# A hybrid decoder step on one core: the reload of keys and queries ahead of the last cached key pages, and the recurrence's operands loaded one a step

## The chip, the cores and the metric

The kernel runs on one core of one Trainium2 chip. The metric is the device time of one execution in microseconds. PE is TensorE (matrix multiply), DVE VectorE, ACT ScalarE, POOL GpSimd and SP SyncE; SP and POOL issue nearly all DMA transfers here, each through a queue of its own.

## The reference, cut to what matters

One layer of a decoder for a prompt of 1024 tokens and 8 samples of one token each, model width 1024:

```
x += 0.5 * SwiGLU_1(RMSNorm(x))
P  = RMSNorm(x) @ W_in            # RWKV-7 columns | q, k, v | two branch gates
A  = RWKV7_time_mix(P_rw)         # state recurrence over the tokens
B  = DiffAttn(P_q, P_k, P_v)      # p1 - lambda*p2, rotary, causal
x += (sigmoid(Ga) * (A @ W_pa) + sigmoid(Gb) * (B @ W_pb)) @ W_out
x += 0.5 * SwiGLU_2(RMSNorm(x))

# a sample's attention reads 2048 cached positions through a page table
kp = cache_k[pt].reshape(n_past, 2 * DA_HEADS, DA_QK)
vp = cache_v[pt].reshape(n_past, DA_HEADS, DA_V)
s = einsum("bqhd,bkhd->bhqk", q, k) * DA_QK ** -0.5
```

All is float32. The sample part has 8 samples of 16 pages, each page 128 positions by 512 numbers (256 KB).

## The kernel before, in words

The program is written by hand for each engine; within an engine instructions stand in the order of the code, and engines meet at semaphores. Activations lie transposed, features on the 128 partitions and 1032 tokens (1024 of the prompt, 8 samples) along them.

Three stages matter here. **The unit loop** computes 30 column blocks ("units", `n` = 0 to 29) of `W_in`: 14 for the recurrence, then 16 for the gates. PE fills PSUM for a unit; DVE reads it out (`tmp<-ps,rstd_mix`, L1903) and thereby frees that PSUM half; for a gate unit ACT then applies the sigmoid and POOL stores it (`gate_save`, L915). In the shadow of the same loop DVE works on the samples' attention scores: a group `f` (0 to 31) is four cached key pages. For each group DVE multiplies by the query (`kq_prod<-key_ring`, L1854) and sums (`score_sums<-kq_prod`, L1858), in the function `score_pages`. The key ring holds two groups. SP loads the pages of the groups of unit `n` two passes later (`groups_of(n - 2)`), a group at a time, when the group two before it has been used (`k_used`). `GROUPS_OF` says how many groups each unit has.

During the unit loop POOL also stores what the recurrence will need later (`kk_save`, `b_save`, `kp_save` and others; the last is `kp_save`, L928, of the fourth head pair at `n` = 26). All of these count on `prep_stored`. Their buffers lie where the rotated keys `Kr` and queries `Q` of the prompt must come back, so these two are reloaded (2064 KB each, `k_rot<-k_save` and `q_rot<-q_save`, L704 and L705) only when `prep_stored` is complete.

**Attention** follows: 32 steps, four head pairs for each of 8 query blocks. The first scores on PE (L2646) need `k_back`, `q_back` and both PSUM halves free. DVE first reduces the sample scores over pages (`rstd<-score_sums`, L1935), then takes the maxima of the first step's scores (L1986 to L1989). From step 4 on, PE weights the cached values in between (`weight_values`, L2623), again in groups `f` of four pages in a ring of three, which SP loads (`value_ring` or `tmp<-in_cache_v`, L685).

**The recurrence** follows attention. Its five operands (kk, b, k, r, v; four tiles of 516 KB each, twenty in all) are loaded back by POOL at the opening of attention, and nothing reads them before attention's last steps. `w_trans_lo` counts the steps whose probability transposes PE has done.

Of the kernel before, what the change touches and what calls it, by code (L numbers as in the profile page):

```python
# [30 lines left out]
HP = 4  # L31
# [100 lines left out]


UNITS = ZT + GT
GROUPS_OF = [0 if n == 0 else 2 if n in (15, 20, 26) else 1 for n in range(UNITS)]
HALF_OF = [n for n in range(UNITS) for _ in range(GROUPS_OF[n])]
PREP_AT = [4, 10, 16, 22]

# [90 lines left out]
def build(nc, A):  # L229

    ctx = ExitStack()
    with ctx:
        ev = Events(nc, ctx)
# [18 lines left out]
        def tiles(name, first, n, dt=F32):  # L252

            return at(name, n * NT, arena + first * TILE, dt)[:, :].rearrange("p (k n) -> p k n", n=NT)
# [48 lines left out]
        Q = tiles("q_rot", 0, HP)  # L303
        Kr = tiles("k_rot", 4, HP)
# [31 lines left out]
        Rf, Kf, Vf = tiles("r_mix", 28, HP), tiles("k_new", 12, HP), tiles("v_mix", 36, HP)  # L336
        KKn = tiles("kk", 16, HP)
        Bf = tiles("b_vec", 20, HP)
# [21 lines left out]
        def both_heads(n):  # L360
# [65 lines left out]
        q_save, k_save, r_save, v_save, kk_save, b_save, kp_save, cum_save = [  # L426
            nc.dram_tensor(name + "_save", (HP, P, NT), F32).ap()
            for name in ("q", "k", "r", "v", "kk", "b", "kp", "cum")]
# [41 lines left out]
        def groups_of(n):  # L470

            return [f for f in range(4 * NS) if HALF_OF[f] == n]
# [146 lines left out]
        def _(sp):  # L619
            def load_unit(s, c, src, nk=KT, second=None):  # L620

                sp.wait_ge(*ev.at(f"w_split{s}", c))
                h = HP
                sp.dma_start(stg[s][:, 0:h, :], src[:, 0:h]).then_inc(ev[f"w_loaded{s}"], 16)
                sp.dma_start(stg[s][:, h:nk, :], src[:, h:nk] if second is None else second)\
                    .then_inc(ev[f"w_loaded{s}"], 16)
# [56 lines left out]
            def cache_page(slot, cache, at, done):  # L683
                page = sp.value_load(ptab[0:1, at], min_val=0, max_val=N_PHYS - 1)
                sp.dma_start(slot, cache[ds(page, 1)].rearrange("a t n -> (a t) n")).then_inc(ev[done], 16)  # L685
# [7 lines left out]
            for n in range(UNITS + 2):  # L693
                if n < UNITS:
                    m = Z_ORDER[n] if n < ZT else GT0 + n - ZT
                    load_unit(n % 2, AT_Z + n // 2, wsrc["w_in"][:, :, m * P:(m + 1) * P])
                for f in groups_of(n - 2):
                    if f >= 2:
                        sp.wait_ge(*ev.at(f"k_used{f % 2}", f // 2))
                    for j in range(4):  # L700
                        cache_page(kring[:, f % 2, j, :], ck, slice(4 * f + j, 4 * f + j + 1), f"key_pages{f % 2}")

            sp.wait_ge(*ev.at("prep_stored", 4 * 16 * HP))
            sp.dma_start(Kr, k_save.rearrange("h p n -> p h n")).then_inc(ev["k_back"], 16)  # L704
            sp.dma_start(Q, q_save.rearrange("h p n -> p h n")).then_inc(ev["q_back"], 16)  # L705
            sp.wait_ge(*ev.at("unit_done0", AT_MERGE))
            sp.wait_ge(*ev.at("unit_done1", AT_MERGE))
            for f in range(4 * NS):
# [42 lines left out]
            for t in range(9):  # L751
                sp.wait_ge(*ev.at(f"y_moved{t % 2}", t // 2 + 1))
                dst = A["y_prompt"][0, t * P:(t + 1) * P, :] if t < 8 else A["y_sample"][:, 0, :]
# [6 lines left out]
        def _(pool):  # L760
# [143 lines left out]
            for n in range(UNITS):  # L904
                p, s = n // 2, n % 2
# [36 lines left out]
            pool.wait_ge(*ev.at("z_stored0", 16 * ring_before(ZT)))  # L942
            pool.wait_ge(*ev.at("z_stored1", 16 * ring_before(ZT + 1)))
            pool.wait_ge(*ev.at("z_rows_stored", 32))
            for dst, src, done in ((KKn, kk_save, "kk_back"), (Bf, b_save, "b_back"), (Kf, kp_save, "kp_back"),
                                   (Rf, r_save, "r_back"), (Vf, v_save, "v_back")):
                for h in range(HP):
                    pool.dma_start(dst[:, h, :], src[h]).then_inc(ev[done], 16)

            def now(c):  # L950
# [2097 lines left out]
```

## Time and profile before

| | us |
|---|---|
| median of 3 runs | 2707.53 |
| lowest and highest | 2705.37 and 2708.22 |
| the profiled execution, its time | 2708.39 |
| its span, first to last instruction | 2706.7 |
| PE busy | 2597.7 (96%) |
| DVE busy | 1700.8 (63%) |

The profile page shows PE busy nearly throughout; the stretch with the most room is attention's opening, from about 1276 us of the span. Times in the rows below are microseconds from the span's start.

### The profile page before, as it was taken

The page shows a single profiled execution, that of the slowest core. Times are in us where ns is not written, and L with a number is a line of the kernel's source. Part 1 is how long each engine was busy: PE and PEld are TensorE (multiplying, and loading weights), DVE is VectorE, ACT ScalarE, POOL GpSimd, SP SyncE. Part 2 cuts the span into 40 slices and gives each one's busy share as a digit, 9 for nine tenths or more (in the row PEclk, how much of TensorE's full clock was granted, in tenths as well). Part 3 has the DMA queues.
Part 4 walks back from the last instruction along what each step waited for, and adds up shares of the span by engine and source line. Part 5 has one row for each costly group of instructions (what it writes and reads, how often), then busy time and mean ns, then how long its engine had stood idle before and what let it go on. Part 6 is the DMA issues. An engine that isn't in the chain of part 4 may idle for free.

```text
span 2706.7 us, 55163 instructions
## 1 busy us (share of the span) xinstructions
PE 2597.7 (96%) x22570; PEld 2463.5 (91%) x22570; DVE 1700.8 (63%) x2054; ACT 804.5 (30%) x1321; POOL 593.5 (22%) x534
## 2 busy tenths in 40 slices
PE   7999999999999999998788999979999999999998
PEld 7999999999999999998355899869999999999998
DVE  5877777422484588677766777575487777663223
ACT  6333333111211222332444232221343333331012
POOL 2333332100010232111101655220023333320000
PEclk8999999999999999999799999879999999999999
DMA  5233332751323545667975101043323333236411
GB/s 196 74 116 98 111 106 64 273 181 55 102 94 106 157 142 173 218 203 252 319 212 162 30 26 31 18 147 109 125 75 110 106 98 111 74 107 208 148 48 71
DMA packets 293399, 342.14 MB, mean 126 GB/s; under 512 B 22324, under 2 KB 217744, under 8 KB 293024
## 3 DMA queue, kind: packets, MB, share of 16 engines
q1 hardware_dynamic: 252960, 189.42, 23.6%
q0 software_dynamic: 40000, 149.17, 15.3%
q8 instruction: 177, 2.90, 0.4%
q14 instruction: 70, 0.57, 0.1%
q10 hardware_dynamic: 192, 0.07, 0.0%
HBM read 254.32 MB, written 84.28 MB: 125 GB/s over the span
## 4 chain that ended last, share of the span: by engine, by line
PE 87%; DVE 8%; DMA 1%; ACT 1%; issue 1%; DVEq 0%; SPq 0%; POOL 0%; ACTq 0%
PE ps L2360 43%; PE ps L2488 29%; PE ps L2726 1%; PE ps L2688 1%; PE ps L2646 1%; PE ps L2741 1%; PE ps L2405 1%; PE ps L2746 1%; PE ps L2623 1%; DMA w_stage<-in_ffn_up 1%; PE ps L2580 1%; PE ps L2773 1%; PE ps L2781 1%; ACT w_trans L1422 1%; PE ps L2671 1%
## 5 line engine op out<-in xcount | busy, mean ns | idle before, releaser
L2360 PE MATMUL ps<-h,w_hi 128*128 128x344 f32 x2112 | 506.4, 324 | 0.0
L2360 PEld LDWEIGHTS ps<-h,w_hi 128*128 128x128 f32 x2112 | 362.1, 188 | 17.4 <-issue 16.7
L2360 PE MATMUL ps<-h,w_lo 128*128 128x344 f32 x1056 | 337.2, 319 | 0.0
L1747 DVE SCALAR_TENSOR_TENSOR x_res<-ps,x_res 128x1032 f32<-128x1032 f32 x48 | 59.2, 1233 | 321.0 <-PE ps L2360 321.0
L2488 PE MATMUL ps<-t,w_hi 128*128 128x258 f32 x1408 | 257.4, 284 | 1.0 <-DVE tmp L1689 0.5
L1166 ACT ACTIVATE w_hi<-w_stage 128x512 fp32r<-128x512 f32 x252 | 157.6, 627 | 317.8 <-PE ps L2488 288.5
L2488 PE MATMUL ps<-t_one,w_hi 128*128 128x258 f32 x1280 | 234.4, 285 | 3.1 <-issue 2.5
L2488 PEld LDWEIGHTS ps<-t,w_hi 128*128 128x128 f32 x1408 | 218.2, 190 | 1.5 <-issue 0.7
L1689 DVE TENSOR_TENSOR tmp<-tmp,ps 128x516 f32<-128x516 f32 x210 | 145.4, 692 | 108.4 <-PE ps L2488 95.3
L1658 DVE TENSOR_TENSOR w_lo<-w_stage,w_hi 128x512 fp32r<-128x512 f32 x252 | 192.0, 762 | 22.7 <-ACT w_hi L1166 0.4
L2488 PEld LDWEIGHTS ps<-t_one,w_hi 128*128 128x128 f32 x1280 | 199.2, 191 | 3.5 <-issue 3.5
L2488 PE MATMUL ps<-t,w_lo 128*128 128x258 f32 x704 | 199.3, 283 | 0.0
L2360 PEld LDWEIGHTS ps<-h,w_lo 128*128 128x128 f32 x1056 | 198.5, 188 | 0.0
L2488 PE MATMUL ps<-b,w_hi 128*128 128x258 f32 x1056 | 192.8, 284 | 0.9 <-DVE tmp L1689 0.9
L2488 PE MATMUL ps<-t_one,w_lo 128*128 128x258 f32 x640 | 181.5, 284 | 0.0
L2488 PE MATMUL ps<-h,w_hi 128*128 128x258 f32 x960 | 174.8, 284 | 1.4 <-ACT tmp L1190 0.8
L2488 PEld LDWEIGHTS ps<-b,w_hi 128*128 128x128 f32 x1056 | 163.4, 190 | 1.1 <-issue 1.1
L793 POOL TENSOR_TENSOR w_stage<-w_stage 128x512 f32<-128x512 f32 x42 | 76.8, 1828 | 346.1 <-DVE w_lo L1658 338.5
L2488 PEld LDWEIGHTS ps<-h,w_hi 128*128 128x128 f32 x960 | 148.4, 190 | 1.9 <-issue 1.8
L2488 PE MATMUL ps<-b,w_lo 128*128 128x258 f32 x528 | 149.3, 283 | 0.0
L1176 ACT ACTIVATE w_hi<-w_stage 128x1024 fp32r<-128x1024 f32 x49 | 51.8, 1056 | 283.8 <-PE ps L2360 262.6
L2488 PE MATMUL ps<-h,w_lo 128*128 128x258 f32 x480 | 135.6, 283 | 0.0
(545 smaller groups left out, 6168.0 us busy)
## 6 DMA issues: line engine op xcount, KB each, us to landing
w_stage<-in_ffn_up SPq DMA_DIRECT2D x176, 256.0 KB, 3.0
key_ring<-in_cache_k SPq DMA_DIRECT2D x128, 256.0 KB, 3.1
value_ring<-in_cache_v SPq DMA_DIRECT2D x88, 256.0 KB, 3.0
w_stage<-in_w_in SPq DMA_DIRECT2D x84, 256.0 KB, 3.3
w_stage<-in_ffn_down SPq DMA_DIRECT2D x80, 256.0 KB, 3.3
g_save<-g_ring POOLq DMA_DIRECT2D x32, 516.0 KB, 4.8
g_save<-g_kept POOLq DMA_DIRECT2D x32, 516.0 KB, 4.6
x_res<-x_save POOLq DMA_DIRECT2D x6, 2064.0 KB, 9.8
```

Source lines behind the costliest of these rows:

```text
L793: nc.gpsimd.tensor_tensor(A12, A12, A11, ALU.subtract).then_inc(ev[of(m, "sum_made")], 1)
L1166: sc.activation(op_slot(whi, n), RAW[i], ACT.Copy).then_inc(ev[of(m, "op_high")], 1)
L1176: sc.activation(whi[b], stg[b], ACT.Copy).then_inc(ev[f"w_high{b}"], 1)
L1422: sc.activation(wT[s][:, 0:n], PSf[:, 4 * 512:4 * 512 + n], ACT.Copy).then_inc(ev["w_moved"], 1)
L1658: in_turn(v.tensor_tensor(op_slot(wlo, n), RAW[n % NPROD], op_slot(whi, n).bitcast(F32), ALU.subtract) .then_inc(ev[of(m, "op_low")], 1))
L1689: in_turn(v.tensor_tensor(halved(out), halved(x), region(bank), ALU.add).then_inc(ev[of(m, "ps_read")], 1))
L1747: in_turn(v.scalar_tensor_tensor(ch3(xm), dense[s], 0.5, ch3(xm), ALU.mult, ALU.add) .then_inc(ev[f"psum_free{s}"], 1))
L2360: last = mm(dense[s][:, j], w[w0][:, k0 + k, :], column(r, k, slice(j * CH, (j + 1) * CH)), start=(k == 0 and n == 0), stop=(k == nk - 1 a ...
L2405: last = mm(dense[s][:, j], w[s][:, k, :], r[:, k, j * CH:(j + 1) * CH], start=(k == 0 and n == 0), stop=(k == KT - 1 and n == 2))
L2488: last = mm(PS[:, bank + c, 0:QUART], w[:, k, :], moving[:, x, k, b], start=(opens and k == 0 and a == 0), stop=(k == 3 and a == 2), skip_ ...
L2580: last = mm(out[:, 0:CH], lw2[q, a * P:(a + 1) * P], zwa[q, third], start=True, stop=True)
L2623: last = mm(PS[32 * j:32 * j + HP, 7, :], VIEW_W[:, b, g, :], value_slot(f)[:, j, :], start=(f % 4 == 0), stop=(f % 4 == 3))
```

## The change

Two edits. First, in SP's loop over units, the two reloads of `Kr` and `Q` with their wait on `prep_stored` move from behind the loop to its pass 30, ahead of the pages of the groups of unit 28; and `GROUPS_OF` takes the last group, `f` = 31, from unit 29 to unit 28, so that unit 28 has groups 30 and 31. Second, each of POOL's twenty loads for the recurrence waits on `w_trans_lo`: the first until PE has done the transposes of three attention steps, each following one until it has done one more, the last until 22.

```diff
-GROUPS_OF = [0 if n == 0 else 2 if n in (15, 20, 26) else 1 for n in range(UNITS)]
+GROUPS_OF = [0 if n in (0, UNITS - 1) else 2 if n in (15, 20, 26, UNITS - 2) else 1 for n in range(UNITS)]
...
             for n in range(UNITS + 2):
                 if n < UNITS:
                     m = Z_ORDER[n] if n < ZT else GT0 + n - ZT
                     load_unit(n % 2, AT_Z + n // 2, wsrc["w_in"][:, :, m * P:(m + 1) * P])
+                if n == UNITS:
+                    sp.wait_ge(*ev.at("prep_stored", 4 * 16 * HP))
+                    sp.dma_start(Kr, k_save.rearrange("h p n -> p h n")).then_inc(ev["k_back"], 16)
+                    sp.dma_start(Q, q_save.rearrange("h p n -> p h n")).then_inc(ev["q_back"], 16)
                 for f in groups_of(n - 2):
...
-            sp.wait_ge(*ev.at("prep_stored", 4 * 16 * HP))
-            sp.dma_start(Kr, k_save.rearrange("h p n -> p h n")).then_inc(ev["k_back"], 16)
-            sp.dma_start(Q, q_save.rearrange("h p n -> p h n")).then_inc(ev["q_back"], 16)
...
-            for dst, src, done in ((KKn, kk_save, "kk_back"), (Bf, b_save, "b_back"), (Kf, kp_save, "kp_back"),
-                                   (Rf, r_save, "r_back"), (Vf, v_save, "v_back")):
+            for i, (dst, src, done) in enumerate(((KKn, kk_save, "kk_back"), (Bf, b_save, "b_back"), (Kf, kp_save, "kp_back"),
+                                                  (Rf, r_save, "r_back"), (Vf, v_save, "v_back"))):
                 for h in range(HP):
+                    pool.wait_ge(*ev.at("w_trans_lo", i * HP + h + 3))
                     pool.dma_start(dst[:, h, :], src[h]).then_inc(ev[done], 16)
```

On SP, at the end of the unit loop, before: the last page of group 31, the two reloads, then the first page of the cached values (the rows between two DMAs are the look-up of a page's number).

```order
L685 DMA key_ring<-in_cache_k 128x512
L704 DMA k_rot<-k_save 128x4x1032
L705 DMA q_rot<-q_save 128x4x1032
L684 TENSOR_LOAD pages
L684 ISA x2
L685 ISA
L685 DMA value_ring<-in_cache_v 128x512
```

On SP in the changed kernel, at the same two reloads (now L699 and L700): the page ahead of them is the last of group 29, the one behind them the first of group 30.

```order
L685 DMA key_ring<-in_cache_k 128x512
L699 DMA k_rot<-k_save 128x4x1032
L700 DMA q_rot<-q_save 128x4x1032
L684 TENSOR_LOAD pages
L684 ISA x2
L685 ISA
L685 DMA key_ring<-in_cache_k 128x512
```

Eight page loads, groups 30 and 31, have moved from ahead of the reloads to behind them.

On DVE, units 28 and 29 and the opening of attention, before (L1903 reads a unit out of PSUM):

```order
L1903 TENSOR_TENSOR tmp<-ps,rstd_mix 128x1032
L1854 TENSOR_TENSOR kq_prod<-key_ring,rstd 128x2048
L1858 TENSOR_REDUCE score_sums<-kq_prod 128x32
L1903 TENSOR_TENSOR tmp<-ps,rstd_mix 128x1032
L1854 TENSOR_TENSOR kq_prod<-key_ring,rstd 128x2048
L1858 TENSOR_REDUCE score_sums<-kq_prod 128x32
L1935 TENSOR_REDUCE rstd<-score_sums 128x64
L1986 TENSOR_TENSOR ps<-ps,const 128x2x128
```

And in the changed kernel, where all lines stand two further down:

```order
L1905 TENSOR_TENSOR tmp<-ps,rstd_mix 128x1032
L1856 TENSOR_TENSOR kq_prod<-key_ring,rstd 128x2048
L1860 TENSOR_REDUCE score_sums<-kq_prod 128x32
L1856 TENSOR_TENSOR kq_prod<-key_ring,rstd 128x2048
L1860 TENSOR_REDUCE score_sums<-kq_prod 128x32
L1905 TENSOR_TENSOR tmp<-ps,rstd_mix 128x1032
L1937 TENSOR_REDUCE rstd<-score_sums 128x64
L1988 TENSOR_TENSOR ps<-ps,const 128x2x128
```

The read-out of unit 29 has moved behind both products of groups 30 and 31. PE, ACT and POOL keep their order; POOL gains waits only.

## Rows read from the trace of the kernel before

**Rows 1.** The page: the chain that ended last, shares of the span.

```profile
PE 87%; DVE 8%; DMA 1%; ACT 1%; issue 1%; DVEq 0%; SPq 0%; POOL 0%; ACTq 0%
```

**Rows 2.** Waits of PE, 1264 to 1330: total us, times, longest.

```profile
PE ps L2646 <- DMA q_rot<-q_save: 6.0, 1, 6.0
...
PE ps L2623 <- DMA value_ring<-in_cache_v: 1.8, 1, 1.8
```

**Rows 3.** Timeline of DVE: start us, us, line, operation [idle before, releaser].

```profile
1266.45 2.29 DVE L1854 TENSOR_TENSOR kq_prod<-key_ring,rstd 128x2048 f32<-128x2048 f32 x1
...
1276.40 1.23 DVE L1903 TENSOR_TENSOR tmp<-ps,rstd_mix 128x1032 f32<-128x1032 f32 x1 [5.28 <-PE ps L2360]
1277.72 2.29 DVE L1854 TENSOR_TENSOR kq_prod<-key_ring,rstd 128x2048 f32<-128x2048 f32 x1
1280.11 2.29 DVE L1858 TENSOR_REDUCE score_sums<-kq_prod 128x32 f32<-128x2048 f32 x1
1282.47 1.99 DVE L1935 TENSOR_REDUCE rstd<-score_sums 128x64 f32<-128x1024 f32 x1
1284.55 0.43 DVE L1986 TENSOR_TENSOR ps<-ps,const 128x256 f32<-128x256 f32 x1
```

**Rows 4.** Timeline of PE, the first scores of attention.

```profile
1282.39 1.23 PE L2646 MATMUL ps<-k_rot,q_rot 64*128 64x128 f32 x8 [6.02 <-DMA q_rot<-q_save]
```

**Rows 5.** Timeline of SP's DMA issues: start us, us, count.

```profile
1266.18 1.68 SPq L704 DMA_DIRECT2D k_rot<-k_save  x1
1267.91 0.51 SPq L705 DMA_DIRECT2D q_rot<-q_save  x1
1277.15 8.71 SPq L685 DMA_DIRECT2D value_ring<-in_cache_v  x8
```

**Rows 6.** DMA issues, 1267.5 to 1268.5: count, KB each, us to landing.

```profile
k_rot<-k_save SPq DMA_DIRECT2D x1, 2064.0 KB, 11.0
q_rot<-q_save SPq DMA_DIRECT2D x1, 2064.0 KB, 14.3
gate_save<-tmp POOLq DMA_DIRECT2D x1, 516.0 KB, 8.2
```

**Rows 7.** DMA issues, 1252.5 to 1259.

```profile
key_ring<-in_cache_k SPq DMA_DIRECT2D x4, 256.0 KB, 3.4
...
kp_save<-k_mix POOLq DMA_DIRECT2D x1, 516.0 KB, 5.6
```

**Rows 8.** DMA issues, 1277 to 1278: the first cached value page.

```profile
value_ring<-in_cache_v SPq DMA_DIRECT2D x1, 256.0 KB, 5.8
```

**Rows 9.** Windows: stretch, us, busy by engine, PEclk, DMA share, GB/s.

```profile
1276.00:1282.00 6.00, 0.36 (x3) 0.08 (x1) 5.42 (x3) 2.79 (x4) 0.53 (x1) 0.83 1.02 419
```

**Rows 10.** Timeline of POOL: the last operand store, and the first four of twenty loads.

```profile
1252.69 0.53 POOL L928 DMA_DIRECT2D kp_save<-k_mix  x1
...
1289.08 2.09 POOL L948 DMA_DIRECT2D kk<-kk_save  x4
```

**Rows 11.** Timeline of ACT, its first probabilities.

```profile
1285.76 0.37 ACT L1398 ACTIVATE probs<-ps,small 128x128 f32<-128x128 f32 x1 [5.27 <-DVE small L1989]
```

**Rows 12.** The chain, 1260 to 1330, in order of time: start us, us, what.

```profile
1317.82 6.60 DMA value_ring<-in_cache_v
1324.46 1.89 PE ps L2623 x8
```

**Rows 13.** DMA issues, 1382 to 1385.4: value pages beside no load of POOL.

```profile
tmp<-in_cache_v SPq DMA_DIRECT2D x4, 256.0 KB, 2.9
```

**Rows 14.** Windows around the second stretch at half clock.

```profile
1320.00:1324.40 4.40, 2.50 (x16) 1.11 (x11) 3.60 (x11) 1.85 (x7) 0.00 (x0) 1.00 1.05 390
1324.40:1327.80 3.40, 3.34 (x14) 1.29 (x14) 1.13 (x3) 0.00 (x0) 0.00 (x0) 0.50 0.93 304
```

**Rows 15.** Timeline of PE: eight value matmuls at full clock, and those of group 17.

```profile
1331.61 1.04 PE L2623 MATMUL ps<-value_ring,s_weights 128*4 128x512 f32 x8
...
1389.94 1.04 PE L2623 MATMUL ps<-tmp,s_weights 128*4 128x512 f32 x8
```

**Rows 16.** Timeline of SP: the issues of group 17's four pages.

```profile
1382.10 3.59 SPq L685 DMA_DIRECT2D tmp<-in_cache_v  x4
```

## The prediction

> **What bounds the kernel now.** I read the page's chain first: 87% of it is PE, so only the places where PE waits can give time back, and the change touches none but attention's opening [rows 1]. Next the waits of PE from 1264 to 1330: one of 6.0 us on the query reload, and one of 1.8 us on a cached value page [rows 2]. They are the two waits at which the two edits aim.
>
> The first has a twin that the wait list hides. PE's first scores start at 1282.39 and take 1.23, so they are done at 1283.6 [rows 4]. But DVE, which must take their maxima, is not free: after unit 29's read-out (1276.40) it works on group 31 (2.29 + 2.29) and on the reduction over pages (1.99), and takes the first maxima at 1284.55 [rows 3]. The chain runs through DVE here. Until DVE's probabilities are ready nothing on PE goes on, so I measure the opening by one landmark: **the start of the first L1986, 1284.55.** What it moves, the end moves.
>
> **Edit 1, its promise.** With group 31 ahead of unit 29's read-out, DVE would have after 1276.40 only the read-out (to the next start 1.32) and the reduction with its gap (1284.55 - 1282.47 = 2.08): landmark at 1279.8, a gain of 4.75, which is the product and sum of one group with gaps (1282.47 - 1277.72). The 5.28 us that DVE idles before unit 29 [rows 3] would take the group's work. That needs the pages of groups 30 and 31 early.
>
> **Edit 1, its price.** Those eight pages now stand behind 4128 KB of reloads in SP's queue. When do the reloads start? SP waits for `prep_stored`, whose last store is issued at 1252.69 and lands 5.6 later [rows 7, 10]: 1258.3. Before, the reload of keys was issued at 1266.18, so it goes out 7.9 earlier. The query reload follows 1.73 behind (1267.91 - 1266.18 [rows 5]), at 1260.0, and lands 14.3 after its issue [rows 6]: 1274.3.
>
> Do pages wait behind it? One row shows such a page: the first value page, issued at 1277.15 [rows 5], took 5.8 us instead of 3.4 or 2.9 [rows 7, 8, 13] and so landed at 1282.95, 0.7 behind the query reload (1267.91 + 14.3 = 1282.2), about the time of its own 256 KB at 419 GB/s (0.63 [rows 9]). That is one line, served in order. A store of POOL in the same stretch landed 8.2 after its issue, ahead of the reloads' end: another queue shares, the same queue does not overtake [rows 6].
>
> So group 30 (four pages, 1.05 MB, 2.5 us at 419 GB/s) lands at 1276.8; in the kernel before DVE had its product begun at 1266.45 [rows 3]. Group 31 lands 2.5 later, 1279.3, while DVE works on group 30. From 1276.8: 4.75 for group 30, 4.75 for group 31, 1.32 for unit 29's read-out, 2.08 for the reduction: **landmark at 1289.7, 5.2 later than before.** Behind DVE's wait for group 30 stands unit 29's read-out, and behind that everything: PE's first scores (they need that PSUM half; 1286.2 + 1.3 = 1287.6, done at 1288.8, just hidden), ACT's last sigmoid and its first probabilities (ACT idles 5.27 before these now [rows 11]), POOL's last gate store. PE's wait in the opening goes from 6.0 to about 11 us, and is laid to DVE.
>
> Bounds of this term. From below: the reloads at 419 GB/s from an idle queue, 10.1 us, after the latency of a lone page without its transfer (3.4 - 0.6 = 2.8), no store beside them: 1271.2, group 30 at 1273.7, landmark 1286.6, a loss of 2.0. From above: two 516 KB gate stores cross the reloads instead of one, 1.3 more, and the pages cross one too, 0.5: a loss of 7.0. I take 5.2, as the two reloads have a measured duration. For the edit to break even group 30 would have to land at 1271.6, the reloads at 1269.1, 10.8 us after the issue of the first; even the lower bound needs 12.9.
>
> A rule of the Trainium skill (DMA: Bandwidth & Descriptors, "Queues, rings and completion order") speaks against this change too: SP owns one row of rings, whose descriptors each DMA engine takes in ring order, while rows of different issuers take turns packet by packet. By it the eight pages cannot start before the reloads' descriptors are drained, so that the loss stands; the same section warns that completion is not strictly first in, first out, which could save a fraction of one page's transfer. The trace agrees as far as the one value page shows.
>
> **Edit 2.** The twenty loads start at 1289.08 now [rows 10] and are 10.6 MB, 25 us at 419 GB/s, so the queues are full till past 1314. Into this fall the pages of value group 3, whose last, issued at 1317.82, takes 6.60 [rows 12] against 2.9 in quiet [rows 13]. PE waits 1.8 for it [rows 2]. With one 516 KB load a step (1.3 us of the queues) the page lands by 1317.82 + 2.9 + 1.3 = 1322.0, before PE wants it (1324.46 - 1.8 = 1322.7): **1.8 gained.** Behind the wait PE ran 3.4 us at half clock (0.50 against 1.00 before it, 1.2 instead of 2.4 GHz [rows 14]): the eight value matmuls took 1.89 there [rows 12] against 1.04 [rows 15], 0.85 more, and the smaller ones about 0.35. Without the wait this may go (1.2) or fall elsewhere (0): I take 0.6. Together 2.4, between 0.5 (if the pages still just miss) and 3.0.
>
> What the spread loads may cost: each lies beside value pages in steps 2 to 21. The tightest group there is 17: last page issued at about 1385.4, landed at 1388.3 [rows 13, 16], used at 1389.94 [rows 15], so 1.6 of slack against at most 1.3 of one load. Nothing. The waits cost POOL nothing: nothing stands behind them but the recurrence, whose operands nothing reads before attention's last steps, and the last load goes out at step 21 of 32.
>
> **Sum.** 5.2 - 2.4 = +2.8 us, bounds -1.0 and +6.5. On the profiled execution (2708.39) that is 2711.2; this execution lies 0.9 above the median of the runs, 2707.53, on which it is 2710.3. I say 2710.5. A measurement of this kernel tells a change of some 0.2%, 5.4 us, from none.
>
> **The rivals.**
> *The pages don't queue (faster).* If reloads and pages shared the bandwidth, group 30 would land in time or nearly: landmark between 1279.8 and about 1283, total gain 4.75 + 2.4 = 7.2 or 1.6 + 2.4 = 4.0; times 2700.4 and 2703.5. For it: the store of POOL did share. Against it: the one value page [rows 8]. Chance 0.12 for over 0.2%, 0.05 for the half-way case.
> *The reloads last longer (slower).* The mechanism is the same queue, with the rate of the reloads pushed down by stores and by the pages' small packets. If the query reload lands at 1276.9 or later, 2.6 behind my estimate, the opening loses 7.8 and the whole 5.4: the point from which it decides. Time 2713.5. For it: two gate stores now fall into the transfer. Against it: the bound of 7.0 above already has both. Chance 0.17.
> *The spread loads keep the value wait alive.* Then edit 2 gives nothing: 2712.7, still within 0.2% (0.06; 0.02 that it costs more and goes over). Against it: the 0.7 and 1.6 us of room above.
> *My forecast*, 0.5 to 5.4 us slower: 0.58.
>
> **How the numbers follow.** Faster 0.12, slower 0.17 + 0.02, the rest, 0.69, the same. The likeliest case by itself spans 2708 to 2713. The range reaches on to 2704 (it leaves out the first rival's 0.12) and to 2714 (it leaves out the upper half of the second, 0.08).
>
> **What the changed profile would show.** The key reload issued at 1258 to 1259 and the query reload landed at 1272 to 1276. The page loads of group 30 with 9 us or more to landing in place of 3.4. DVE idle some 9 us before the product of group 30, with the DMA as releaser, none before unit 29's read-out. PE's wait on the query reload gone, one of 10 to 11 us on DVE in its place, the first L1988 (before: L1986) at 1287 to 1291. POOL's loads one a step; no PE wait on value pages; PE at half clock through the opening still. I would be wrong if group 30's pages landed before 1271.6, or if DVE's order let unit 29's read-out go ahead.

## The result and the profile after

The changed kernel takes 2713.73 us (median of 8 runs, 2712.18 to 2718.45); before, 2707.44 (8 runs, 2702.33 to 2711.16). The medians lie 6.3 us apart (0.23%). The ratio on record, 1.003 with a 95% interval of [1.002, 1.004], agrees with the means, which lie 7.5 us apart. The prediction was 2710.5 and no difference that can be measured; the kernel has become slower, clear of the noise.

**Attention's opening.** Timeline of DVE in the changed kernel, units 28 and 29 (start us, us, line, operation [idle before, releaser]; lines stand two further down than before). PE's last unit ends at 1273.65 here, 1276.36 before.

```profile
1262.41 1.23 DVE L1905 TENSOR_TENSOR tmp<-ps,rstd_mix 128x1032 f32<-128x1032 f32 x1 [0.98 <-PE ps L2362]
1274.74 2.29 DVE L1856 TENSOR_TENSOR kq_prod<-key_ring,rstd 128x2048 f32<-128x2048 f32 x1 [11.09 <-DMA key_ring<-in_cache_k]
...
1284.30 1.23 DVE L1905 TENSOR_TENSOR tmp<-ps,rstd_mix 128x1032 f32<-128x1032 f32 x1
1285.62 2.00 DVE L1937 TENSOR_REDUCE rstd<-score_sums 128x64 f32<-128x1024 f32 x1
1287.71 0.43 DVE L1988 TENSOR_TENSOR ps<-ps,const 128x256 f32<-128x256 f32 x1
```

Against [rows 3]: DVE waits 11.09 us for group 30's pages. The read-out of unit 29 starts at 1284.30, 10.6 us after PE's last matmul, where it started at once before. The landmark, the first maxima, comes at 1287.71, which is 14.06 us after PE's last matmul of the units; before it was 8.2. The opening has lost 5.9 us.

DMA issues from 1256.7 to 1257.2 (count, KB each, us to landing):

```profile
gate_save<-tmp POOLq DMA_DIRECT2D x1, 516.0 KB, 7.8
key_ring<-in_cache_k SPq DMA_DIRECT2D x1, 256.0 KB, 15.0
```

The first page of group 30, issued at 1256.75, takes 15.0 us where a page took 3.4 [rows 7]. It lands at 1271.75, 0.2 us behind the query reload (issued at 1255.48, 16.1 us to landing): the pages have queued behind it.

Waits of PE in the changed kernel, 1264 to 1486 (total us, times, longest):

```profile
PE ps L2648 <- issue: 12.1, 1, 12.1
PE ps L2625 <- DMA tmp<-in_cache_v: 4.2, 2, 2.7
```

The wait on the query reload [rows 2] is gone, and PE stands idle 12.1 us before its first scores; the releaser is written as "issue", but the matmul starts 0.2 us after unit 29's read-out ends (1284.30 + 1.23), the PSUM half that it needs. The wait on value group 3 is gone too; two others stand in its place, in later groups. The same two waits in PE's timeline, at groups 5 and 17:

```profile
1337.61 1.04 PE L2625 MATMUL ps<-tmp,s_weights 128*4 128x512 f32 x8 [2.70 <-DMA tmp<-in_cache_v]
...
1395.70 1.04 PE L2625 MATMUL ps<-tmp,s_weights 128*4 128x512 f32 x8 [1.53 <-DMA tmp<-in_cache_v]
```

A third item is in DVE's wait list, 1262 to 1296, and was not in the prediction:

```profile
DVE kq_prod L1856 <- DMA key_ring<-in_cache_k: 11.1, 1, 11.1
DVE rstd L1948 <- POOL rstd L938: 1.5, 1, 1.5
```

L938 is POOL's all-reduce, which takes the maximum of the page maxima over all partitions and gives it back to DVE. Before, DVE waited 0.16 us there.

**Stage by stage.** I cut attention at the same events in both traces: PE's last unit, first maxima, transposes of step 3, value groups 3, 7, 17 and 27, end of attention. Windows of before (stretch, us, busy time of PE, its weight loads, DVE, ACT and POOL, granted clock, DMA share, GB/s):

```profile
1276.40:1284.55 8.15, 1.23 (x8) 0.96 (x8) 7.80 (x5) 2.79 (x4) 0.53 (x1) 0.72 1.03 415
1284.55:1305.79 21.24, 9.37 (x31) 4.75 (x31) 17.10 (x44) 7.21 (x31) 11.55 (x22) 0.50 0.98 363
1305.79:1324.46 18.67, 14.52 (x71) 5.99 (x72) 13.13 (x35) 7.51 (x30) 0.00 (x0) 0.77 1.03 404
1324.46:1349.18 24.72, 22.28 (x141) 11.40 (x141) 17.33 (x41) 11.79 (x38) 0.00 (x0) 0.93 0.79 233
1349.18:1389.94 40.76, 35.87 (x264) 21.31 (x266) 26.80 (x60) 20.61 (x55) 0.00 (x0) 1.00 0.71 216
```

And of the changed kernel:

```profile
1273.70:1287.71 14.01, 1.23 (x8) 0.96 (x8) 12.39 (x6) 2.13 (x2) 0.53 (x1) 0.63 0.66 200
1287.71:1310.28 22.57, 9.38 (x31) 4.75 (x32) 17.05 (x44) 7.89 (x34) 1.70 (x3) 0.50 0.37 114
1310.28:1326.95 16.67, 14.29 (x72) 5.82 (x72) 11.61 (x31) 7.04 (x29) 2.12 (x4) 0.76 0.58 188
1326.95:1353.22 26.27, 22.36 (x141) 11.70 (x141) 18.85 (x45) 12.36 (x41) 3.18 (x6) 0.94 0.99 345
1353.22:1395.70 42.48, 36.06 (x264) 21.21 (x263) 28.41 (x62) 20.63 (x55) 3.71 (x7) 1.00 0.91 302
```

Compare the second column, the length of each stretch: +5.9 (DVE without pages), +1.3 (the all-reduce), -2.0 (group 3 no longer waited for), +1.6 and +1.7 (the new value waits, at groups 5 and 17). The last column moves with them: the transfers that filled 363 and 404 GB/s now stand beside the value pages, 345 and 302 GB/s. From group 17 to 27 both need 51.23 us, after which another 1.1 is lost, which I have not traced. Attention as a whole is 9.5 us longer in this execution; before it the execution is 2.7 us ahead and behind it another 2.9, so that the spans differ by 3.9 only. These last two parts do the same work in both kernels: two executions differ by some 3 us where nothing was changed. So I take the sums from the medians.

### The profile page after: what moved, and what is told of

It reads as the page before. It is cut to its first block, busy times and chain, and to the rows that moved or that the text cites. A ratio compares the mean times of both kernels' runs of the same rounds, so it can differ in the third digit from the quotient of the medians.

```text
span 2710.6 us, 55163 instructions
## 1 busy us (share of the span) xinstructions
PE 2595.6 (96%) x22570; PEld 2461.1 (91%) x22570; DVE 1705.2 (63%) x2054; ACT 805.8 (30%) x1321; POOL 592.5 (22%) x534
## 4 chain that ended last, share of the span: by engine, by line
PE 85%; DVE 8%; DMA 2%; issue 1%; ACT 1%; SPq 1%; POOL 0%; DVEq 0%; ACTq 0%; POOLq 0%
PE ps L2362 41%; PE ps L2490 29%; PE ps L2728 1%; PE ps L2690 1%; PE ps L2743 1%; PE ps L2648 1%; PE ps L2748 1%; PE ps L2407 1%; PE ps L2625 1%; DMA w_stage<-in_ffn_up 1%; PE ps L2582 1%; PE ps L2783 1%; PE ps L2775 1%; DMA key_ring<-in_cache_k 1%; PE ps L2673 1%
```

## The experiments

All were timed against the kernel before in five rounds, 10 or 11 runs each; "opening" is the time from PE's last unit matmul to DVE's first maxima, 8.2 us before and 14.1 in the changed kernel. An interval of a ratio is some 0.1% to either side, 2.5 us, so terms of 1 or 2 us rest on the traces.

**Edit 1 alone**: the changed kernel without the twenty waits.

```diff
-                    pool.wait_ge(*ev.at("w_trans_lo", i * HP + h + 3))
```

> Edit 1 without edit 2. Theory Q (queue): group 30's pages stand behind the reloads, so DVE takes the first maxima 14.0 us after PE's last unit as in the changed kernel (8.15 before), and the page maximum on POOL comes 1.3 us later still; the value wait of group 3 stays, as the burst of operand loads stays. Time 6 to 8 us over before, about 2714. Rival C (clock): the loss is made by PE's longer stretch at half clock after its longer idle; then the same kernel would show DVE's chain unchanged in length and PE's matmuls longer, and the time would be under 3 us over before.

Measured: 2713.08 us, ratio 1.0024 [1.0015, 1.0033], that is +6.0 on 2707.1. Opening 14.4. Waits of DVE, 1264 to 1300:

```profile
DVE kq_prod L1855 <- DMA key_ring<-in_cache_k: 11.5, 1, 11.5
DVE rstd L1947 <- POOL rstd L938: 1.1, 1, 1.1
```

PE's wait on value group 3 stays (1.73). So edit 1 by itself makes a loss as large as the whole, through DVE. PE's stretch at half clock is longer (41.0 us in place of 34.1), but nearly all of that lies ahead of the first maxima, where PE is idle; from them on it lasts 30.0 us here and 29.6 before, and DVE's chain is longer. The clock rival falls.

**Edit 2 alone**: before, with the twenty waits.

> Edit 2 without edit 1. Theory S (spread loads collide): the wait on group 3 (1.8 us) goes, and new waits of PE on value pages come where a load of 516 KB lies beside them, 2.7 us at group 5 and 1.5 at group 17 as in the changed kernel; net between -1 and +3 us, and the opening unchanged at 8.15 us. Rival: these waits were there only because edit 1 had put the steps out of time with the pages; then edit 2 alone is 2 to 3 us faster than before and has no wait over 0.5 us on a value page.

Measured: 2706.17, ratio 1.0001 [0.9992, 1.0010], no difference that can be told (between -2.2 and +2.7 us). The opening is as before, 8.2; there is no wait on group 3, and group 17 is not waited for either; but PE's timeline at group 5 shows:

```profile
1331.12 1.04 PE L2624 MATMUL ps<-tmp,s_weights 128*4 128x512 f32 x8 [2.81 <-DMA tmp<-in_cache_v]
```

The rival, that the new waits belong to edit 1, falls for group 5; the wait on group 17 was seen in the changed kernel alone. The wait on group 3 has moved two groups on.

**The group's move alone**: before, with group 31 in unit 28 and the reloads behind all pages.

```diff
-GROUPS_OF = [0 if n == 0 else 2 if n in (15, 20, 26) else 1 for n in range(UNITS)]
+GROUPS_OF = [0 if n in (0, UNITS - 1) else 2 if n in (15, 20, 26, UNITS - 2) else 1 for n in range(UNITS)]
```

> Only the move of group 31 to unit 28; the reloads stay behind all key pages. Theory Q: pages land as before, DVE has groups 30 and 31 done before unit 29 ends, and the bound becomes the reloads: they land 5.8 us after PE's last matmul as before, scores take 1.2, so the first maxima come 7.3 us after it in place of 8.15: 0.9 us gained, time the same within 0.1%. If instead the last gate store and the page maximum decide, nothing is gained.

Measured: 2706.24, ratio 0.9997 [0.9988, 1.0007]. Opening 6.9: 1.3 gained, and DVE now idles in it:

```profile
1278.02 1.99 DVE L1935 TENSOR_REDUCE rstd<-score_sums 128x64 f32<-128x1024 f32 x1
1283.58 0.43 DVE L1986 TENSOR_TENSOR ps<-ps,const 128x256 f32<-128x256 f32 x1 [3.57 <-PE ps L2646]
```

The move by itself shortens the opening and the reloads then bind: DVE idles 3.57 us for PE's first scores, and these wait 6.1 us for the query reload. By group 17 of this execution the 1.3 us are gone, and PE had one further stretch of 3.4 us at half clock on the way.

**The last gate store behind the all-reduce**, on the changed kernel.

```diff
                 if n >= ZT:
                     pool.wait_ge(*ev.at(f"gate_made{s}", p - ZPAIRS + 1))
-                    pool.dma_start(g_save[n - ZT], T[:, s, :]).then_inc(ev[f"gate_saved{s}"], 16)
+                    if n < UNITS - 1:
+                        pool.dma_start(g_save[n - ZT], T[:, s, :]).then_inc(ev[f"gate_saved{s}"], 16)
...
             nc.gpsimd.partition_all_reduce(smax, smaxp, P, bass.bass_isa.ReduceOp.max).then_inc(ev["s_max_all"], 1)
+            pool.dma_start(g_save[GT - 1], T[:, 1, :]).then_inc(ev["gate_saved1"], 16)
```

> The changed kernel, with POOL's store of the last gate unit put behind the page maximum (the all-reduce) instead of ahead of it. Theory P: the store, issued 0.6 us before DVE hands over the page maxima, holds POOL, and so the all-reduce comes 6.6 us after DVE's hand-over instead of 5.3; without it 5.3 or less, DVE's wait of 1.5 us on POOL gone, and 1.3 us gained on the changed kernel. Rival: the all-reduce takes what it takes, and the wait stays at 1.5 us.

Measured: 2711.71, ratio 1.0023 [1.0014, 1.0033]. The opening is 14.8. Waits of DVE, 1280 to 1300:

```profile
DVE kq_prod L1858 <- DMA key_ring<-in_cache_k: 11.8, 1, 11.8
DVE rstd L1950 <- issue: 0.2, 1, 0.2
```

The wait on POOL is gone. DVE comes to this line 5.35 us after it has handed the page maxima over, and no longer finds them missing; with the store ahead it got them 6.6 us after. That is the 1.3 us of the stage table. The gain rests on the traces: the interval of this ratio overlaps that of the change, and PE still waits 3.6 us on value pages, at groups 5, 6 and 9.

What holds the all-reduce can be seen on POOL. Its line has two configuration records, MODIFY_POOL_CONFIG, which come right behind whatever POOL issued last. First the changed kernel, with the store ahead, then this run:

```profile
1287.01 0.53 POOL L916 DMA_DIRECT2D gate_save<-tmp  x1 [21.34 <-ACT tmp L1368]
L938 POOLq MODIFY_POOL_CONFIG  x2: 33/35/37, 1287.6 to 1287.6; - x2
1293.68 0.54 POOL L938 PARTITION_ALL_REDUCE rstd<-rstd  x1 [6.13 <-issue]
```

```profile
L939 POOLq MODIFY_POOL_CONFIG  x2: 33/35/37, 1268.3 to 1268.3; - x2
1291.16 0.55 POOL L939 PARTITION_ALL_REDUCE rstd<-rstd  x1 [22.90 <-DVE rstd L1939]
```

In the changed kernel the records come at 1287.6, together with DVE's hand-over (1287.62), and the all-reduce starts 6.1 us later. In the kernel before they come at 1279.7, DVE hands over at 1284.46, and the all-reduce starts at 1287.90 and is done 1.2 us before DVE asks for it. With the store behind, the records come at 1268.3; the all-reduce starts 0.25 us after DVE's hand-over (1290.91) and its record ends 0.8 us after it. So it is not the hand-over that it waits for where the store is ahead: over the ten kernels of that kind, 5.7 to 8.4 us pass from these records to the all-reduce. A late store makes the records late, and with them the all-reduce. Whether it is they or the store ahead of them that takes the time, no run tells apart: a store stands ahead of them in every kernel.

**The reloads ahead, group 31 left in unit 29**, and without the twenty waits.

> Only the reloads ahead of the pages of groups 30 and 31, group 31 still in unit 29, operand loads in a burst as before. Theory Q: group 30 lands 1.4 us after PE's last matmul and holds unit 29's read-out, then group 31 and the page maximum: the same chain of DVE as with group 31 in unit 28, first maxima 14.4 us after PE's last matmul, time about 6 us over before. Rival: the loss comes from the eight products lying ahead of the read-out; then with group 31 behind it the PSUM half is freed 4.7 us sooner and the loss is about 1.5 us.

Measured: 2710.15, ratio 1.0014 [1.0005, 1.0023], +2.9. The opening is 14.8 us, as the queue theory has it, for DVE waits 11.85 us for group 30 ahead of the read-out all the same. The rival is refuted by the opening, not by the time: the total expected was 6, and half of that is missing. In the trace two things come back. Unit 29's read-out lies between the groups, so the last gate store is issued early enough and the all-reduce is not held (0.16). And POOL's operand loads, which follow the all-reduce, begin 2.0 us after the first maxima, where before they began 4.5 after them (1289.08 against 1284.55, [rows 3, 10]), so that their burst meets the steps earlier: no wait at group 3. Against edit 1 alone, these two are 1.1 and 1.7 us.

**The reloads on POOL's queue**, group 31 in unit 28; the reloads on SP go, and the operand loads are a burst as before.

```diff
...
+                if n == 27:
+                    pool.wait_ge(*ev.at("prep_stored", 4 * 16 * HP))
+                    pool.dma_start(Kr, k_save.rearrange("h p n -> p h n")).then_inc(ev["k_back"], 16)
+                    pool.dma_start(Q, q_save.rearrange("h p n -> p h n")).then_inc(ev["q_back"], 16)
```

> Group 31 in unit 28, and both reloads issued by POOL right behind the gate store of unit 27, on POOL's queue, so that the key pages have SP's queue for themselves; operand loads in a burst as before. Theory Q: the pages of groups 30 and 31 land at most 3 us later than before, DVE does both before unit 29 ends; the reloads land about 0 us after PE's last matmul; first maxima 3.4 us after it in place of 8.15. The last gate store then again stands just ahead of the page maximum on POOL (1.3 us given back). Gain 3 to 5 us, time about 2703. Rival: all queues share one bandwidth, so pages beside the reloads are as late as behind them, and DVE waits 5 us or more: no gain.

Measured: 2710.43, ratio 1.0015 [1.0006, 1.0025], slower where I expected 3 to 5 us of gain. Group 30's pages are there in time. The last page of group 31, issued at 1264.30:

```profile
key_ring<-in_cache_k SPq DMA_DIRECT2D x1, 256.0 KB, 11.3
```

On a queue of its own the page still takes 11.3 us while the reloads run; the query reload takes 18.5. The page lands at 1275.6, 2 us ahead of the query reload (1259.08 + 18.5), where on one queue it landed behind it: the two queues do share. DVE waits 6.3 us for group 31, and the opening is 9.3. The rival was right that DVE would wait 5 us or more and nothing be gained: from 1264 to 1276 the DMA engines are busy throughout (388 to 411 GB/s), so that, as I read it, only the order in which the bytes go can be chosen. It was wrong that the pages would be as late as behind the reloads: the opening lies nearer to before (8.2) than to the change (14.1).

**Operand loads at later steps**: before, each load waiting on a number of a list.

```diff
+            LOAD_AT = [12, 13, 14, 15, 16, 17, 18, 18, 21, 22, 23, 23, 24, 25, 26, 26, 28, 28, 29, 30]
...
+                    pool.wait_ge(*ev.at("w_trans_lo", LOAD_AT[i * HP + h]))
```

> Before, with the twenty operand loads spread over later steps: each waits on a count of w_trans_lo of 12 to 18, 21 to 26 or 28 to 30, none in steps 2 to 10, where the page issues of SP keep pace with the steps and leave no room. Theory S: the wait on group 3 goes and none comes in its place; 2 to 3 us gained on before, about 2704.5. Rival: SP's issue rate (four pages in 4.4 us) makes PE wait in steps 5 to 9 anyway, by 1 us or more in all, and the gain stays under 1 us as with the loads from step 2 on.

Measured: 2704.89, ratio 0.9993 [0.9984, 1.0002], not to be told from before. Group 3's wait is gone, but against my expectation another comes, at group 9, beside the first of the loads:

```profile
1351.86 1.47 PE L2625 MATMUL ps<-value_ring,s_weights 128*4 128x512 f32 x8 [2.65 <-DMA value_ring<-in_cache_v]
```

**Reloads on POOL, store behind, loads at these later steps, together**, group 31 in unit 28.

> Together: group 31 in unit 28, reloads on POOL's queue, the last gate store behind the page maximum, operand loads at the late steps. If the three terms are right and add up: 4.7 us in the opening and 2 to 3 us at the value pages, 2700 to 2701, 0.25% under before. If the clock takes it back or a new wait on value pages comes in steps 4 to 9 (all steps come sooner against the pages, which wait for a used ring slot): 2704 or more.

Measured: 2705.93, ratio 0.9994 [0.9985, 1.0003]: opening 9.4, and 1.11 us at group 9. I expected 2700 to 2701. The first term has the wrong sign: the opening is 1.2 us longer than before instead of 4.7 shorter. Whether the others add up the noise does not tell.

**The reload in pieces**: before, with group 31 in unit 28; the reloads stay behind all key pages, but the 256 columns that the first eight steps read go ahead of the rest.

```diff
...
             sp.wait_ge(*ev.at("prep_stored", 4 * 16 * HP))
-            sp.dma_start(Kr, k_save.rearrange("h p n -> p h n")).then_inc(ev["k_back"], 16)
-            sp.dma_start(Q, q_save.rearrange("h p n -> p h n")).then_inc(ev["q_back"], 16)
+            sp.dma_start(Kr[:, :, 0:2 * P], k_save[:, :, 0:2 * P].rearrange("h p n -> p h n")).then_inc(ev["k_back"], 16)
+            sp.dma_start(Q[:, :, 0:2 * P], q_save[:, :, 0:2 * P].rearrange("h p n -> p h n")).then_inc(ev["q_back"], 16)
+            sp.dma_start(Kr[:, :, 2 * P:NT], k_save[:, :, 2 * P:NT].rearrange("h p n -> p h n")).then_inc(ev["kq_rest"], 16)
+            sp.dma_start(Q[:, :, 2 * P:NT], q_save[:, :, 2 * P:NT].rearrange("h p n -> p h n")).then_inc(ev["kq_rest"], 16)
...
+                if step == 2 * HP:
+                    pe.wait_ge(*ev.at("kq_rest", 32))
```

> Group 31 in unit 28, reloads on SP's queue behind all key pages as before, but in pieces: first the 256 columns of keys and queries that steps 0 to 7 read (1 MB), then the rest (3.2 MB), for which PE waits at step 8. Theory: the full reload was all that bound the opening with group 31 moved (6.9 us to the first maxima); the first pieces land before PE's last matmul ends, the first maxima come 3.4 us after it, the page maximum on POOL then ends 0.6 us after the store and gives 1.3 back. 3.4 us gained in the opening, of which a wait on value pages of group 3 or the clock may take a part: 2703 to 2706. Rival: DVE's hand-over of the page maximum and POOL's 8.7 us for it with the store ahead bind instead: DVE waits 2 us or more on POOL and under 2.5 us are gained.

Measured: 2707.01, ratio 1.0006 [0.9997, 1.0015]. The opening is 3.45 us, all 4.75 of the promise. Nothing of it arrives, as DVE's and PE's timelines show:

```profile
1287.52 0.23 DVE L1948 TENSOR_TENSOR rstd<-rstd,s_self 128x64 f32<-128x64 f32 x1 [2.27 <-POOL rstd L939]
```

```profile
1323.56 1.04 PE L2625 MATMUL ps<-value_ring,s_weights 128*4 128x512 f32 x8 [3.34 <-DMA value_ring<-in_cache_v]
```

DVE gives 2.3 us back to the all-reduce, and PE waits 3.34 at group 3 in place of 1.77. The operand loads stand behind the all-reduce on POOL, so the burst begins 7.9 us after the first maxima instead of 4.5 (first operand load at 1288.11, first maxima at 1280.26) and lasts further into the steps. The six kernels with the burst go this way, roughly: with the first load 2.0, 3.8, 4.5, 6.7, 6.7 and 7.9 us after the first maxima, PE waits at group 3 for 0, 1.6, 1.8, 1.7, 2.1 and 3.3 us.

**All three together**, group 31 in unit 28: pieces, store behind, and `LOAD_AT = [15, 15, 16, 16, 17, 18, 21, 22, 22, 23, 24, 24, 25, 26, 28, 28, 29, 29, 30, 30]`.

> The split reload, the last gate store behind the page maximum, and the operand loads from count 15 of w_trans_lo on, none in steps 2 to 13. If all add up: 4.7 us in the opening, 1.8 us of the wait on group 3 and about 0.8 of the half-clock stretch behind it: 7 us, 2700. If SP's issue of four pages in 4.4 us now sets the pace of steps 4 to 13, the value waits come back at any group there and 2 to 4 us of it are lost: 2702 to 2704.

Measured: **2699.84 us, ratio 0.9977 [0.9968, 0.9986]**, 6.5 us under before and 0.5% under the change. DVE's timeline:

```profile
1276.12 1.23 DVE L1909 TENSOR_TENSOR tmp<-ps,rstd_mix 128x1032 f32<-128x1032 f32 x1 [0.54 <-PE ps L2366]
1277.44 2.00 DVE L1941 TENSOR_REDUCE rstd<-score_sums 128x64 f32<-128x1024 f32 x1
1279.53 0.43 DVE L1992 TENSOR_TENSOR ps<-ps,const 128x256 f32<-128x256 f32 x1
```

The read-out, the reduction and the first maxima follow each other without a gap. PE waits on value pages 1.7 us in all, at groups 7, 12 and 14.

**The later loads alone**: before, with this second list.

> Before, with the operand loads from count 15 of w_trans_lo on (three more steps of peace than in the run with late loads, whose wait on group 9 was 2.65 us with the first of the loads beside its pages). Theory S: no wait over 0.5 us on a value page in steps 4 to 13, 2.5 to 4 us gained on before: 2703.5 to 2705. Rival (SP's issue rate): groups 7 to 10 wait 1 us or more in all even with the queues quiet.

Measured: 2704.43, ratio 0.9994 [0.9985, 1.0003]. Waits of PE for a DMA, 1276 to 1486:

```profile
PE ps L2648 <- DMA q_rot<-q_save: 6.2, 1, 6.2
PE ps L2625 <- DMA value_ring<-in_cache_v: 0.4, 1, 0.4
```

The value waits are gone and the profile's attention is 1.9 us shorter, but its time cannot be told from no change by itself.

**All three, with the change's own spacing of the loads**, one a step from the third on.

```diff
-                    pool.wait_ge(*ev.at("w_trans_lo", LOAD_AT[i * HP + h]))
+                    pool.wait_ge(*ev.at("w_trans_lo", i * HP + h + 3))
```

> The fastest version so far (split reload, last gate store behind the page maximum), but with the operand loads one a step from count 3 on, as the change has them. Theory S: loads beside the pages of groups 3 to 11, whose issue on SP has no room, make PE wait 3 us or more in all on value pages and bring a further stretch at half clock: 3 to 5 us slower than with the loads from count 15 on, about 2703.5. Rival: it is enough that the burst is gone; then the time stays within 1.5 us of 2700.

Measured: 2701.45, ratio 0.9982 [0.9973, 0.9991]. PE waits 1.72 us at group 5 and 0.6 at groups 7 and 9. The 3 to 5 us that I expected over the later list are 1.6, and the intervals overlap; in the two traces attention is even 1.6 us shorter here (199.4 against 200.9 us from PE's last unit to the recurrence). So the rival stands: with the short opening it is enough that the burst is gone, and where the loads go after that can't be told. There is no further stretch at half clock, as there was behind group 5's wait in the change and in edit 2 alone; why not here is open.

## Why the prediction was wrong

*"The same queue does not overtake"* was right and well sized. Predicted: key reload issued at 1258 to 1259, in this execution 1255.05, 18.6 us before PE's last unit ends as expected (1276.4 - 1258.3 = 18.1). Predicted "some 9" us of DVE idle, though its own times give 10.3 (1276.8 - 1266.45); measured 11.09. Opening loss 5.2 between 2.0 and 7.0, measured 5.9: group 30's last page was 3.1 us behind the query reload (1274.7 against 1271.6) where 2.5 were allowed for it. Edit 1 alone showed a loss of 6.0 us by itself. The rule of the Trainium skill (DMA: Bandwidth & Descriptors, "Queues, rings and completion order") said the same of SP's queue; of its other half, rows of different issuers taking turns, the run with the reloads on POOL's queue shows the price, 11.3 us for a page beside them.

*"Behind that everything ... POOL's last gate store"*: the prediction named the store but gave it no price, and it did not name the all-reduce behind it at all. That step failed. The read-out is late, so the store is issued 0.6 us before DVE hands over the page maxima (1287.01 against 1287.62) instead of 5.3 us before, and the all-reduce, which starts 5.7 to 8.4 us after the records behind the store, is late by 1.3 us. Moving the store behind it took the wait away.

*Edit 2, "1.8 gained", with 0.6 of clock behind it, and "What the spread loads may cost ... Nothing"* is the step that turned the answer, for with it went the 2.4 us that the prediction took off. The gain is there (2.0 in the stage table). The cost, called nothing, is 1.6 and 1.7 us. Two assumptions were wrong. First, a load beside a page group was to cost its own 1.3 us; DMA issues from 1327.7 to 1331.1 in the changed kernel show four pages of group 5 at 5.5 against 2.9 in quiet [rows 13]:

```profile
b_vec<-b_save POOLq DMA_DIRECT2D x2, 516.0 KB, 6.7
tmp<-in_cache_v SPq DMA_DIRECT2D x4, 256.0 KB, 5.5
```

The median page is 2.6 us later, twice the estimate, with two loads falling into one group's issue. Second, I read the room of each group from a trace in which PE had waited at group 3. That wait, and the half clock behind it, were themselves a source of the room: SP issues four pages in 4.4 us, as fast as the steps go, so without them the steps run up to the pages. SP's timeline in the changed kernel (start us, us, operation, count):

```profile
1319.02 7.97 SPq L685 DMA_DIRECT2D value_ring<-in_cache_v  x8
1327.76 3.59 SPq L685 DMA_DIRECT2D tmp<-in_cache_v  x4
1332.13 8.33 SPq L685 DMA_DIRECT2D value_ring<-in_cache_v  x8
```

Groups 3, 4, 5 and on are issued 4.4 us apart with hardly a pause. At group 5 the account closes. Before, its last page was issued at 1326.57, landed 3.0 later and was used at 1333.91: 4.3 us of room. In the change it is issued 3.5 us nearer to its use, for group 3 is reached sooner without its wait (2.0) and the steps behind it no longer run at half clock (1.5). And it takes 6.5 us to land: 3.5 more. 4.3 - 3.5 - 3.5 = -2.7, the wait of 2.70. By time, edit 2 alone is worth 0 and not -2.4, which lies just outside its interval (-2.2 to +2.7).

The sum becomes 5.9 + 1.3 + 0 = 7.2 against 6.3 by the medians and 7.5 by the means. Against my 2.8 that is 2.4 for edit 2, 1.3 for the all-reduce and 0.7 for the opening. The half clock *"may go (1.2) or fall elsewhere (0)"*: it fell elsewhere, 3.4 us at half clock behind group 5's wait in place of group 3's (granted clock 0.50):

```profile
1338.80:1342.20 3.40, 3.40 (x11) 1.85 (x10) 0.41 (x1) 1.57 (x6) 0.00 (x0) 0.50 1.02 388
```

The rival that ended slower gave 2713.5, near the measured time, but that is luck, for its cause was another: it asked the reloads to last 2.6 us longer, and in the change they landed at 1271.6, 2.1 us before PE's last unit ended, as forecast (1274.3 against 1276.4).

What stays open: whether and why the run with the reloads alone is better than edit 1 alone. The medians say 3.1 us, but the intervals overlap. The absent waits on POOL and at group 3 would account for 1.1 and 1.7; no run undid just one of these in it. And the run with the store behind shows attention up to value group 27 shorter than the change by 5.0 us in the trace, of which 1.3 are explained; its median is 2.0 us lower.

## What to carry to other kernels

A transfer moved ahead in a queue pushes back whatever it passes; price it by the consumer of what is passed, and by what stands behind that consumer's wait on its own engine. If only part of a large reload is needed first, let that part go first: with group 31 moved and 1 MB of pieces at the head of the reload, behind the pages, the opening gained the whole 4.75 us, where the full 4 MB ahead of the pages cost 5.9. Room measured behind a wait vanishes when the wait does; read it again from a run without the wait. And test edits that hand their gain to each other together: the pieces alone and the later loads alone were each within 0.1% of before, and with the store moved they made 6.5 us in one kernel.

## What the runs showed of the hardware that was not expected

POOL's all-reduce started 5.7 to 8.4 us after the configuration records of its own line in the ten kernels where these came behind the last gate store, though the store's own instruction takes 0.53 us and the all-reduce's 0.54. In the four where the store came behind it, the records had come 11 us or more ahead, and the all-reduce's record ended 0.8 us after DVE's hand-over. DVE waited for it only where the store was late or the opening short: 1.1 us in edit 1 alone and with the reloads on POOL's queue, 1.5 in the change and 2.3 with the reload in pieces.

A page of 256 KB took 11.3 us beside two reloads of 2064 KB on another queue and landed 2 us ahead of the second of them; on their own queue, behind them, it took 15.0 us and landed 0.2 us after them. The query reload took 18.5 us in the first case and 16.1 in the second.
